# Hybrid attention and pooling layer on one core: ScalarE's queue also reads two columns of every row of the first K tile's weights

## The reference, cut to what matters

```python
hn   = rmsnorm(x, pre_norm_gain)              # x: 512 tokens x 2048 features, float32
proj = hn @ w_in                              # -> q | k | v | gate_a | u_pool | gate_b
y_a  = stick_breaking(q, k, v) * silu(g_a)    # 8 heads x 128
y_b  = multiscale_pool(u_b) * silu(g_b)       # 4 groups x 256
out  = concat(y_a, y_b) @ w_out
x    = x + rmsnorm(out, post_norm_gain)
```

## Time and profile before

| | us |
|---|---|
| median of 3 runs | 715.9 (715.43 to 716.0) |
| the profiled execution, its own time | 715.07 |
| span of the profiled execution | 713.2 |
| TensorE busy (share of the span) | 704.1 (99%) |
| VectorE busy | 587.3 (82%) |
| ScalarE busy | 439.8 (62%) |
| GpSimd busy | 76.1 (11%) |

### The profile page before, as it was taken

The page is one execution under the profiler, slowest core; times in us unless marked ns, Lnnn a source line. Parts: engine busy times, 40 slices in busy tenths (PEclk is TensorE's granted clock), DMA queues, the critical chain, the costliest instruction groups (busy, mean ns, idle before and its releaser), DMA issues.

```text
span 713.2 us, 9845 instructions
## 1 busy us (share of the span) xinstructions
PE 704.1 (99%) x3696; PEld 607.5 (85%) x3696; DVE 587.3 (82%) x756; ACT 439.8 (62%) x598; POOL 76.1 (11%) x94
## 2 busy tenths in 40 slices
PE   8999999999999999999999999999999999999995
PEld 7888888888888888888888888888888888888884
DVE  3499977998789898898897978898898984376787
ACT  4765576666776756777766677766688434253561
POOL 0000000210020110011120011030000000001001
PEclk9999999999999999999999999999999999999999
DMA  8965446567756666656765665656654308467985
GB/s 292 392 199 140 128 118 174 152 171 199 177 117 178 159 194 177 168 145 161 193 156 159 178 173 165 165 147 176 170 168 177 119 24 242 119 176 221 273 331 236
DMA packets 38542, 128.57 MB, mean 180 GB/s; under 512 B 4320, under 2 KB 5344, under 8 KB 37600
## 3 DMA queue, kind: packets, MB, share of 16 engines
q1 hardware_dynamic: 31440, 102.78, 42.1%
q0 software_dynamic: 6912, 25.17, 20.7%
q10 hardware_dynamic: 144, 0.01, 0.0%
HBM read 123.74 MB, written 4.19 MB: 179 GB/s over the span
## 4 chain that ended last, share of the span: by engine, by line
PE 96%; DVE 2%; issue 0%; POOL 0%; DVEq 0%; ACT 0%; ACTq 0%
PE ps L1931 36%; PE ps L1939 19%; PE ps L1875 11%; PE ps L1842 9%; PE ps L1843 9%; PE ps L1841 9%; PE ps L1975 1%; PE ps L1974 1%; DVE mix L1733 1%; PE ps L1907 1%; DVE mix L1635 0%; PE ps L1858 0%; PE ps L1866 0%; PE ps L1868 0%; DVE mix L1663 0%
## 5 line engine op out<-in xcount | busy, mean ns | idle before, releaser
L1931 PE MATMUL ps<-a_ops,w_hi 128*128 128x512 f32 x1120 | 270.8, 391 | 0.0
L1931 PEld LDWEIGHTS ps<-a_ops,w_hi 128*128 128x128 f32 x1120 | 205.6, 188 | 39.4
L674 ACT ACTIVATE w_hi<-raw 128x1024 fp32r<-128x1024 f32 x155 | 163.2, 1055 | 64.7 <-PE ps L1931 35.6
L1147 DVE TENSOR_TENSOR raw_lo<-raw,w_hi 128x1024 fp32r<-128x1024 f32 x155 | 188.8, 1224 | 17.1 <-ACT w_hi L674 16.8
L1939 PEld LDWEIGHTS ps<-a_ops,raw_lo 128*128 128x128 f32 x1120 | 145.7, 191 | 6.3
L1939 PE MATMUL ps<-a_ops,raw_lo 128*128 128x256 f32 x1120 | 149.9, 283 | 0.0
L1788 POOL DMA_DIRECT2D raw<-w_heads x40 | 34.9, 873 | 313.6 <-DMA raw<-w_heads 248.2
L1841 PE MATMUL ps<-w_hi,a_ops 128*128 128x512 f32 x160 | 62.4, 390 | 0.0
L1843 PE MATMUL ps<-w_hi,a_ops 128*128 128x512 f32 x160 | 62.3, 390 | 0.0
L1842 PE MATMUL ps<-raw_lo,a_ops 128*128 128x512 f32 x136 | 53.0, 390 | 0.0
L1162 DVE TENSOR_TENSOR raw<-raw 128x1024 f32<-128x1024 f32 x40 | 48.7, 1218 | 1.0 <-PE ps L1843 1.0
(11 more groups left out here) (232 smaller groups left out, 1027.8 us busy)
## 6 DMA issues: line engine op xcount, KB each, us to landing
raw<-w_heads SPq DMA_DIRECT2D x100, 512.0 KB, 4.2
raw<-w_heads POOLq DMA_DIRECT2D x40, 512.0 KB, 5.7
raw<-w_out SPq DMA_DIRECT2D x35, 512.0 KB, 5.1
raw<-w_v SPq DMA_DIRECT2D x15, 512.0 KB, 10.1
x_rows<-x SPq DMA_DIRECT2D x6, 1024.0 KB, 12.0
mix<-xT SPq DMA_DIRECT2D x16, 256.0 KB, 10.0
out<-mix SPq DMA_DIRECT2D x8, 512.0 KB, 2.7
raw_more<-w_out SPq DMA_DIRECT2D x6, 512.0 KB, 7.6
```

The source lines that it names most:

```text
L674: act.activation(hi_slot(g), raw_slot(raw, slot), ACT.Copy).then_inc(w_hi_done, 1)
L1147: dve.tensor_tensor(raw_slot(raw_lo, slot), raw_slot(raw, slot), hi_slot(g).bitcast(F32), ALU.subtract).then_inc(w_split, 1)
L1931: mm = pe.matmul(dst, hi[:, k * P:(k + 1) * P], a_ops[:, a:a + SEQ], start=k == 0 and p in (0, 1, 5), stop=stop and k == KH - 1, skip_grou ...
```

## The change

A tile of 128 rows by four floats (`first_columns`) and a semaphore (`columns_loaded`) are added. ScalarE's queue, after the load of the gain and ahead of the table load, issues two more loads: columns 0 and 1 of all 128 rows of `w_v[0]`, and the same of `w_v[4]`, which are 8 bytes from each row that W0a and W0b read. No instruction uses what lands in the tile. As its last instruction ScalarE waits until both loads have landed. All other instructions stand as they were, in the same order.

```diff
--- before.py
+++ after.py
@@ -184,6 +184,7 @@
         out_rstd = sb("out_rstd", [P, TT])
         not_first = sb("not_first", [P, 1])
         neg_not_first = sb("neg_not_first", [P, 1])
+        first_columns = sb("first_columns", [P, 4])
 
 
         half, row_root = ms_col[:, 0:1], ss_col[:, 0:1]
@@ -278,6 +279,7 @@
             return bank(FORM_BANK[p] + i)
 
         gain_loaded = sem("gain_loaded")
+        columns_loaded = sem("columns_loaded")
         scale_loaded = sem("scale_loaded")
         rows_gain_loaded = sem("rows_gain_loaded")
         x_loaded = [sem(f"x_loaded{i}") for i in range(V_STEPS)]
@@ -645,6 +647,9 @@
         @block.scalar
         def _(act):
             act.dma_start(pre_gain_col[:, :], pre_gain).then_inc(gain_loaded, 16)
+
+            for g in range(2):
+                act.dma_start(first_columns[:, 2 * g:2 * g + 2], w_v[g * KK][:, 0:2]).then_inc(columns_loaded, 16)
             act.preload_act_table_set("natural_log_exp_and_others")
 
             def x_hi_of(i):
@@ -1120,6 +1125,7 @@
                         rows_square(*FORM_TILES[n])
             for n in range(4, 8):
                 rows_square(*FORM_TILES[n])
+            act.wait_ge(columns_loaded, 32)
 
         @block.vector
         def _(dve):
```

## The result

The change makes the kernel slower: 719.09 us as the median of six runs (718.83 to 719.62), against 715.58 us for six runs of the kernel before beside it. The ratio is 1.0051, with a 95% interval of 1.0040 to 1.0061. That is 3.5 us more. The prediction gave 716.0 us and a range up to 717.6.

The account below looks back on a forecast made before the run. TensorE, busy 99% of the span, was taken to bound the kernel. Terms 0 + 0.1 + 0 + 0 = +0.1 us on the profiled 715.07 gave 715.2, so a median of 716.0 us; range 715.2 to 717.6.

Parts of the forecast that it names:

- The change part by part: Section costing the issues, packets, W0's reads, end wait and later arrivals one by one, in all +0.1 us.
- what follows step 0: Second K tile's weights, copied with 1.0 us of slack: 0.19 us of packets is hidden there, cost 0.
- Issues and table load: ScalarE's queue at the start: two issues delay the table load by 0.89 us, hidden before x_hi, cost 0.
- Packets: DMA engines at the start: 288 added packets, 0.19 us on each engine, 0.1 us taken, bounds 0 and 0.19.
- What the reads do to W0: W0's own packets at the start: effect taken as 0, bounds -0.19 and +1.7 us.
- Rival 1: At W0's loads: the reads make W0's way free, -0.19 us, median 715.7 us; chance 0.20.
- Rival 2: First weight load of line 1858: the reads hold W0 back, up to 1.7 us, 717.6 us; chance 0.13.
- late change of pace: Step 0: a hole in TensorE's work may delay the rise to 0.23 us per matmul, adding 4 us: 721.6.
- The last wait: End of ScalarE's queue: the loads landed some 700 us before, nothing stands behind the wait, cost 0.
- the first sign: Start of the V stage: the first matmul of line 1875 moving by over 0.3 us would prove the prediction wrong.

Follow-up runs that it names:

- e2: The change with its tile allocated behind all other tensors, so that no other tensor moves: 715.85 us, ratio 1.0006.
- e11: The change with its tile allocated ahead of all others, so all tensors lie 32 bytes further: 715.85 us, ratio 1.0008.
- e1: The kernel before plus only the tile where the change puts it, without reads, semaphore or last wait: 719.14 us, ratio 1.0050.
- e5: The kernel before with 32 bytes of padding ahead of all tensors, no reads, no distance between tensors changed: 715.41 us, ratio 1.0002.
- e4: The kernel before with 32 bytes put in ahead of x_lo0, so x_lo moves and x_hi stays, no reads: 716.40 us, ratio 1.0014.
- e8: The kernel before with small tiles shared, so the tensors the change moves lie 128 bytes nearer, no reads: 718.45 us, ratio 1.0042.
- e12: The kernel before with four one-column constants in one tile, so the same tensors lie 96 bytes nearer, no reads: 719.02 us, ratio 1.0049.

## Why the prediction was wrong

**The step that failed** is in "The change part by part": it goes through the issues, the packets, W0's own packets, the last wait and what follows step 0, and has no entry for the tile. The place of 46 tensors was thereby costed at nothing, without a word. The sentence it rests on, that a load at the start can matter "in one way only: by moving the moment at which TensorE's unbroken run of useful matmuls begins", holds for the load (e2, e11), but the change is a load and a tile. All other instructions stand as they were, but not the addresses that they use, and so the change touches more than the first products. The unbroken run itself became slower: 2.4 us in the V stage, some 1.3 us in later stages (there the groups with `o_hi` and `o_lo`, whose operands the move also split, went from 389 to 395 ns; not every later group was followed). e1 shows the tile alone to be worth 3.65 us, as much as the whole result of 3.5 us.

**Issues and table load: right.** The issues took 0.94 us (0.89 predicted), the table load ran from 2.21 to 3.49, and `x_hi` started at 3.65 as before.

**Packets: number right, place wrong, size open.** 288 packets were predicted and came. They were put at 2.5 to 3.5 us, but 203 of them moved between 3.4 and 6.3 us. 0.1 us was taken for them, with 0.19 as the bound; W0b was 0.23 us later on the mean, within the spread of the runs without reads, and the medians of e2 and e11 lie 0.4 and 0.6 us up, with intervals that hold both 0 and 0.19. So the size of this term is not settled.

**What the reads do to W0: as taken, nothing.** Neither the 1.7 us of relief nor 1.7 us of further stall showed. Rival 1 has fallen: with the reads W0 came no sooner on the mean of four profiles. Why the stretch from 3.4 to 6.3 us is slow stays open; reading two columns of the rows did not cure it, for after the change the same stretch moved 121 GB/s, and 135 before.

**Rival 2 named the right side for the wrong reason.** Its place, the first weight load of step 0, was not late: the first matmul started at 6.27 us (6.28 before). The fifth, which needs W0b, started at 8.07 us (7.76 before). A late change of pace did not come with the change: the pace rose earlier. **The last wait: right**, no piece of the chain after.

The prediction called itself wrong "if the first matmul of line 1875 moves by over 0.3 us, or if the end moves when that start doesn't". By the letter the first sign came, for the start moved by 0.44 us; but without reads that start alone spreads over 0.6 us. What told was the end: it moved by 4.1 us, 3.7 us more than the start.

## What to carry to other kernels

In a kernel that allocates its tensors one after another, a new tile, however small, moves every tensor behind it; in a kernel bound by TensorE, compare the nanoseconds of one matmul in equal groups before looking for a wait. Keep the distance between a matmul's weights and its moving operand what it was (here a multiple of 256 bytes): put small tiles behind everything, or in front of everything, or pad to 256. Other shapes and types than the float32 matmuls of this kernel were not tried. And when a change adds a buffer together with its work, run the buffer alone: it took one line here and was the whole answer.

## What the runs showed of the hardware that was not expected

A stream of matmuls of 512 columns, each with new weights, ran at 0.2267 us when weights and moving operand lay a multiple of 256 bytes apart, and at 0.2334, 0.2333, 0.2334, 0.2289 and 0.2334 us at distances of 32, 160, 128, 192 and 224 modulo 256. The start of an operand by itself did not matter (e5). The mechanism was not tested. That the next weights are read while the present operand streams would fit: the page of the profile shows PEld busy beside PE, and in e4's trace the distance from the start of the last matmul with `x_hi` to that of the first with the moved `x_lo` is already 235 instead of 227 ns (medians over 14 steps). But it is still 231 ns from the first matmul behind `x_lo` to the second, and the scores above show that more than a matmul's own two operands has a part. The Trainium skill, *SBUF — State Buffer*, section "A bandwidth-pool intuition that's wrong (but worth ruling out)", gives TensorE a second, independent read port for its weights. Taken alone, that would leave the distance no part; here it has one, of 6.7 ns in 227.

The moment at which TensorE's pace doubles is not fixed: ten warm matmuls took 4.64 us before and 4.01 after. The reads are not needed for the earlier rise: in e8 and e12, which have none, the ten took 4.04 and 4.05 us. And two reads of 1 KB are not quick: from issue to landing they took 5.2 us, the two 256 KB loads beside them 5.0:

```profile
raw<-w_v SPq DMA_DIRECT2D x2, 256.0 KB, 5.0
first_columns<-w_v ACTq DMA_DIRECT2D x2, 1.0 KB, 5.2
```
